# One decoder layer on one core: small TensorE products moved inside dense matmul pieces, a routing step with other instructions and an index table converted in two parts

## Chip, cores and metric

The kernel is written for one Trainium2 chip and runs on one of its cores. The metric is the time of one execution on the device, in microseconds (us); a kernel's time is the median of its runs. TensorE is called PE here, VectorE DVE, ScalarE ACT, GpSimd POOL and SyncE SP. "fp32r" is TensorE's one-pass format for 32-bit numbers; plain fp32 products take two recorded instructions each.

## The reference, cut to what matters

One layer over 1088 tokens (1024 of a prompt, 8 x 8 of a decoding batch), width 1024: a projection into eight groups of 256 columns, four mixers, an output projection with residual, then a routed mixture of 32 experts of which each token uses two.

```python
h = rmsnorm(x, g_mix)
z = h @ w_in                                  # 1024 -> 2048
a_b, a_c, a_x, p_x, c_a, c_g, d_u, d_v = split(z, 8)
y_a = a_b * causal_dwconv(a_c * a_x, state_a, conv_a_w)       # 3 taps
y_p = multiscale_pool(p_x, ...)               # causal means over 2, 4, 8, 16 rows, minus x, then 64x64 products, times pool_scale
y_c = silu(layernorm(causal_dwconv(c_a * sigmoid(c_g), state_c, conv_c_w) + b))   # 31 taps
y_d = d_u * chunk_spatial_mix(layernorm(d_v)) # 128 x 128 causal product per chunk and head
x = x + concat([y_a, y_p, y_c, y_d]) @ w_out
h = rmsnorm(x, g_ffn)
# hier_moe: top group of 4, then top 2 of its 8 experts
lg = h @ rg_w + rg_b;  p_top, g_idx = top_k(softmax(lg), 1)
le_sel = (h @ re_w + re_b).reshape(n, 4, 8)[g_idx]
v2, e_idx = top_k(le_sel, 2);  w2 = softmax(v2) * p_top
x = x + sum_k w2[k] * (silu(h @ w_gate[e_k]) * (h @ w_up[e_k])) @ w_down[e_k]
y = rmsnorm(x, g_final)
```

The last rows of the inputs of mixers A, B and C, and the normed v rows of mixer D, are outputs too (the "states").

## The kernel before, in words

Each engine has one program, in an order written out by hand; semaphores join them, and every engine works strictly in its own order. Tokens are cut in nine tiles of 128 rows (the last has 64).

**Input projection.** The weight matrix comes in 16 pieces of 128 columns, in the order of the list PIECES: cg0, ca0, cg1, ca1, v0, v1, du0, du1, p0, p1, ac0, ax0, ac1, ax1, ab0, ab1. For each piece SP loads it, ACT copies the high part (`part_hi`), DVE computes the low part (`part_lo`), and PE runs `z(p)`: 8 steps over the contraction, each of 9 matmuls (three products of high and low parts, three ranges of tokens), 72 in all. A `behind` function, if there is one, is called after each of the 8 steps. ACT or DVE empties the result (`empty`, `glu`, `a_input`, `a_gate`), and `z(p)` can only start when the piece two before in the same banks has been emptied.

**Small work between the pieces.** Spatial products of mixer D (`spatial`, nine, behind the steps of `z(9)`), transposes of the states (`tails`, which need ACT's `tail_copy`), pool products (`pool_product`, three ranges for each of two channel halves c), channel means and variances of mixer C (`over_channels`), all in plain fp32. They share two PSUM banks in the order of the list M_USES: a product may open its bank when the product two before it in the list has been read out. DVE meanwhile computes the 31-tap convolution of mixer C, one instruction of 1024 columns per tap (`taps_c(c, k0, k1)`, line 1148), the pool sums (`pooled(c)`: running sums, a selection, then means minus input) and, for the second channel half, `sample_c(1)`; `conv_ready` is signalled after them.

**Output projection and router phase.** Weights of the output are split in the same way (`part_hi`, `part_lo` of NPIECE + c). PE's loop runs i over tiles: the first half of `project(i)` (24 matmuls of 512 columns), transposes of normed tile i-1, the running counts `cum` of tile i-2 (two fp32 products of 32 columns: `upper` and `ones` times `msum`), the second half, the router logits of tile i-1 (8 fp32 products of 40 columns), and `table_add(i-2)`. DVE does `mix_lo`, `places`, `table_parts`, `residual`, `normed`, `route`. `route` picks group and experts by MAX8 and FIND_INDEX8; `places` gives each token its row in the expert's list; `table_parts` makes the factors from which `table_add` builds the table of token indices, 32 experts by 9 columns, in PSUM. After the last addition DVE turns the table to integers (lines 1444 to 1446), signals `idx_ready`, and POOL starts the first gather.

**Experts and end.** SP loads three weight blocks at once, after the last normed tile, and the others once the third gather has landed. PE takes block after block: transposes of the gathered tokens, gate and up products, a transpose, down products; at most 16 extra blocks follow for experts with over 128 tokens (three with this data). POOL gathers and scatters. At the end DVE adds the two gated rows of each token and norms.

## Time and profile before

| | us |
|---|---|
| median of 3 runs | 693.06 |
| lowest, highest | 691.35, 695.70 |
| the profiled execution | 691.8 |
| its span in the profile | 690.0 |
| PE busy in the span | 585.3 (85%) |
| DVE busy | 371.3 (54%) |
| ACT busy | 203.4 (29%) |
| POOL busy | 97.1 (14%) |

The profiled execution's time is 1.8 us above its span and 1.26 us under the median. Busy shares are averages over stages: input projection to about 258 us, output projection and router to about 406 us, experts to 636 us, then the final sums. Times in the rows are counted from the start of the span.

### The profile page before, as it was taken

The page shows a single profiled execution, that of the slowest core. Times are in us where ns is not written, and L with a number is a line of the kernel's source. Part 1 is how long each engine was busy: PE and PEld are TensorE (multiplying, and loading weights), DVE is VectorE, ACT ScalarE, POOL GpSimd, SP SyncE. Part 2 cuts the span into 40 slices and gives each one's busy share as a digit, 9 for nine tenths or more (in the row PEclk, how much of TensorE's full clock was granted, in tenths as well). Part 3 has the DMA queues.
Part 4 walks back from the last instruction along what each step waited for, and adds up shares of the span by engine and source line. Part 5 has one row for each costly group of instructions (what it writes and reads, how often), then busy time and mean ns, then how long its engine had stood idle before and what let it go on. Part 6 is the DMA issues. An engine that isn't in the chain of part 4 may idle for free. (4 is left out here: it accounts for less than half of the span.)

```text
span 690.0 us, 9547 instructions
## 1 busy us (share of the span) xinstructions
PE 585.3 (85%) x3149; PEld 498.7 (72%) x3149; DVE 371.3 (54%) x668; ACT 203.4 (29%) x349; POOL 97.1 (14%) x150
## 2 busy tenths in 40 slices
PE   3899999994999998999999629999999999998000
PEld 2899999972998896888887417777777787775000
DVE  4929988999993676466566570111111111111497
ACT  6632113220323263211311103333333333332232
POOL 4300002000000000000000211233232333231000
PEclk9999999997999999999999758999999999999555
DMA  9623111120223333100010368998899999892694
GB/s 320 122 93 65 44 32 30 53 60 0 62 79 121 115 108 123 62 30 32 31 61 32 120 228 265 336 327 294 303 340 315 344 326 360 295 334 100 260 352 167
DMA packets 51439, 116.27 MB, mean 169 GB/s; under 512 B 8434, under 2 KB 26743, under 8 KB 50295
## 3 DMA queue, kind: packets, MB, share of 16 engines
q1 hardware_dynamic: 42899, 92.82, 39.8%
q0 software_dynamic: 6656, 17.84, 7.3%
q10 hardware_dynamic: 1828, 4.96, 2.0%
q8 instruction: 25, 0.41, 0.3%
q14 instruction: 31, 0.25, 0.1%
HBM read 99.75 MB, written 20.68 MB: 175 GB/s over the span
## 5 line engine op out<-in xcount | busy, mean ns | idle before, releaser
L1600 PE MATMUL ps<-at_hT,at_ring 128*128 128x384 f32 x936 | 160.3, 330 | 0.0
L1600 PEld LDWEIGHTS ps<-at_hT,at_ring 128*128 128x128 f32 x936 | 155.5, 188 | 1.2 <-issue 1.2
L1833 PE MATMUL ps<-at_wexp,at_hTm 128*128 128x256 f32 x560 | 128.0, 382 | 0.0
L1833 PEld LDWEIGHTS ps<-at_wexp,at_hTm 128*128 128x128 f32 x560 | 104.6, 192 | 13.3 <-issue 0.3
L1756 PE MATMUL ps<-at_hT,at_mring 128*128 128x512 f32 (+1 forms) x432 | 102.3, 392 | 2.4 <-DVE at_mring L1300 1.7
L1756 PEld LDWEIGHTS ps<-at_hT,at_mring 128*128 128x128 f32 (+1 forms) x432 | 77.4, 182 | 21.5 <-issue 2.1
L1479 DVE TENSOR_TENSOR at_actv<-at_sg,ps 128x128 f32<-128x128 f32 x35 | 10.0, 287 | 148.6 <-ACT at_sg L832 148.6
L1148 DVE SCALAR_TENSOR_TENSOR at_mixT<-at_uc,sb_par,at_mixT 128x1024 f32<-128x1024 f32 x60 | 77.4, 1289 | 2.1
L1853 PE MATMUL ps<-at_wexp,at_actT 128*128 128x512 f32 x140 | 65.9, 593 | 0.9 <-ACT at_actT L840 0.9
L1819 PEld LDWEIGHTS ps<-sb_ident,at_xg 128*128 128x128 f32 x280 | 37.4, 193 | 26.2 <-issue 22.5
L543 ACT ACTIVATE at_wk<-at_x 128x1024 f32<-128x1024 f32 (+1 forms) x27 | 28.6, 1058 | 85.0 <-DVE at_x L1353 52.4
L1819 PE MATMUL ps<-sb_ident,at_xg 128*128 128x128 f32 x280 | 38.8, 284 | 9.3 <-DMA at_xg<-scratch_h,at_gidxs 7.9
L1487 DVE COPY at_outb<-ps 128x512 f32<-128x512 f32 x35 | 24.2, 691 | 41.5 <-PE ps L1853 41.5
L1023 POOL DMA_INDIRECT scratch_out<-at_outb,at_tab x32 | 30.4, 948 | 103.1 <-DVE at_outb L1487 99.6
L825 ACT ACTIVATE at_hTm<-ps 128x1024 f32<-128x1024 f32 x35 | 35.8, 1024 | 18.5 <-PE ps L1819 18.5
L1853 PEld LDWEIGHTS ps<-at_wexp,at_actT 128*128 128x128 f32 x140 | 26.5, 190 | 20.0 <-issue 16.7
L1091 DVE SCALAR_TENSOR_TENSOR at_wk<-at_x,sb_rs,sb_gain 128x1024 f32<-128x1024 f32 (+1 forms) x18 | 23.1, 1284 | 31.6 <-POOL sb_rs L926 24.9
L1008 POOL DMA_INDIRECT at_xg<-scratch_h,at_gidxs x32 | 31.6, 989 | 54.2 <-issue 37.3
L924 POOL TENSOR_SCALAR sb_ss<-sb_ss 128x1 f32<-128x1 f32 (+1 forms) x18 | 5.2, 290 | 231.4 <-ACT at_wk L543 231.1
L1556 PE MATMUL ps<-sb_ident,at_wk 128*128 128x128 f32 (+1 forms) x144 | 23.6, 318 | 16.2 <-DVE at_wk L1091 12.4
L849 ACT ACTIVATE at_outb<-ps 128x512 f32<-128x512 f32 x35 | 20.9, 597 | 52.0 <-PE ps L1853 52.0
L1556 PEld LDWEIGHTS ps<-sb_ident,at_wk 128*128 128x128 f32 (+1 forms) x144 | 21.2, 200 | 19.1 <-issue 13.3
(214 smaller groups left out, 580.3 us busy)
## 6 DMA issues: line engine op xcount, KB each, us to landing
at_wexp<-in_expert_w_gate SPq DMA_DIRECT2D x35, 512.0 KB, 7.4
at_wexp<-in_expert_w_up SPq DMA_DIRECT2D x35, 512.0 KB, 4.5
at_wexp<-in_expert_w_down SPq DMA_DIRECT2D x35, 512.0 KB, 6.0
at_x<-in_x_prompt SPq DMA_DIRECT2D x16, 512.0 KB, 6.1
at_raw<-in_w_in SPq DMA_DIRECT2D x16, 512.0 KB, 4.1
at_opair<-scratch_out SPq DMA_DIRECT2D x8, 1024.0 KB, 11.8
scratch_h<-at_wk SPq DMA_DIRECT2D x8, 512.0 KB, 2.6
out_y_prompt<-at_x ACTq DMA_DIRECT2D x8, 512.0 KB, 3.2
```

Of the source, the lines that this page charges most:

```text
L543: do(A(wk[0:n, 2, 0:D], x1[0:n, i, :], ACT.Square, accum_out=ss[0:n, norm, i:i + 1]), s["sq_done"])
L825: nc.scalar.activation(hTm[:, j % 2, :, :], src, ACT.Copy).then_inc(s["htm_ready"], 1)
L1008: g.indirect_dma_start(xg[0:n, b % XG, :], None, hs, bass.IndirectOffsetOnAxis(ap=index[0:n, :], axis=0), bounds_check=last_token, oob_is_ ...
L1023: g.indirect_dma_start(orow, bass.IndirectOffsetOnAxis(ap=index[0:n, :], axis=0), outb[0:n, b % 2, :], None, bounds_check=last_pair, oob_i ...
L1148: do(stt(y, x, par[:, c, k:k + 1], y, ALU.mult, ALU.add))
L1487: v.tensor_copy(outb[:, j % 2, 512:D], ps[:, 6, :]).then_inc(s["ob_dve"], 1)
L1556: mm = pe.transpose(ps[:, banks + k // 4, k % 4 * P:k % 4 * P + n], wk[0:n, i % 2, 0:D].rearrange("p (q k) -> p k q", k=KC)[:, k, :], iden ...
L1600: mm = pe.matmul(ps[:, bank + r, 0:t1 - t0], w[:, wpart, k * P:(k + 1) * P], hT[:, hpart, k, t0:t1], start=(m, wpart, hpart) == (0, 0, 0), ...
L1756: mm = pe.matmul(ps[0:n, b + r, :], mring[:, 1 - i % 2, mpart, k * P:k * P + n], wo[:, wpart, k, r * 512:(r + 1) * 512], start=(c, mpart, ...
L1819: mm = pe.transpose(ps[:, k // 4, k % 4 * P:(k % 4 + 1) * P], xg[:, j % XG, :].rearrange("p (q k) -> p k q", k=KC)[:, k, :], ident[:])
L1833: mm = pe.matmul(ps[:, 2 + j % 2, 0:2 * FF].rearrange("p (g f) -> p g f", g=2), hTm[:, j % 2, k, :], w[:, :, k, :], start=k == 0, stop=k = ...
L1853: mm = pe.matmul(ps[:, 5 + r, :], actT[:, j % 2, :], wexp[:, j % LAP, q:q + 512], start=True, stop=True)
```

## The change

- PE: pool products, state transposes, means and variances are no longer issued between the pieces, but by `behind` functions after given steps of z(10), z(12), z(13), z(14) and z(15). Their order among themselves is the same.
- DVE: `pooled(c)` is cut in `pool_sums` and `pool_means`. For c = 0 both move up between the spatial steps; only three taps stay there (13 to 15) instead of eight; taps 16 to 19 come before the second pool, 20 to 30 after it.
- PE: `project` is cut in four quarters. In iterations before the last the order is that of before. In the last one (tile 8) the logits of tile 7 come between the third and the fourth quarter; after the loop: counts of tile 7, transposes, logits of tile 8, table of 7, counts of 8, table of 8.
- DVE: in the last iterations `route(7)` comes before `residual(8)`, `places(7)` right after it, `table_parts(7)` ahead of `route(8)`.
- `route`: instead of multiplying by the group's one-hot and reducing to 8 values, it adds -1e30 to the other groups and takes MAX8 and FIND_INDEX8 over all 32; one reduction and one index computation go.
- Counts: `upper`, `msum` and a new copy `ones_r` (made by POOL after output-weight part 3) are fp32r, so that the two count products are one-pass.
- The table is converted in two parts: the first three experts' 27 columns, with a signal, then the other 261; POOL waits for the second before its fourth gather.

```diff
-        upper = sb("upper", [P, P])
+        upper = sb("upper", [P, P], F32R)
-        msum = sb("msum", [P, 2, NE])
+        msum = sb("msum", [P, 2, NE], F32R)
...
+            lo_wait(pool, NPIECE + 3)
+            do(g.tensor_copy(ones_r[:], ones[:]), s["ones_ready"])
...
+                if b == 0:
+                    pool.wait_ge(s["idx_ready"], 2)
...
-            zf_wait(dve, "du1")
-            for i in range(TILES):
-                spatial(i)
-                if i < LAST:
-                    taps_c(1, 13 + i, 14 + i)
-            def pooled(c):
-                n = HP + NP + SB * (HP + ST)
-                row = [wk[:, r, :] for r in range(3)]
+            def pool_rows(c):
+                return [wk[:, n, :] for n in range(3)], HP + NP + SB * (HP + ST)
+            def pool_sums(c):
...
+                return dst
+            def pool_means(c, dst):
...
-            pooled(0)
+            zf_wait(dve, "du1")
+            spatial(0)
+            spatial(1)
+            taps_c(1, 13, 14)
+            spatial(2)
+            sums = pool_sums(0)
+            spatial(3)
+            spatial(4)
+            pool_means(0, sums)
+            spatial(5)
+            spatial(6)
+            taps_c(1, 14, 15)
+            spatial(7)
+            taps_c(1, 15, 16)
+            spatial(LAST)
             part_lo(11)
-            taps_c(1, 21, 24)
+            taps_c(1, 16, 20)
             part_lo(12)
-            pooled(1)
-            taps_c(1, 24, 31)
+            pool_means(1, pool_sums(1))
+            taps_c(1, 20, 31)
...
-                do(ts(goh[q, :], io4[q, :], gidx[q, :], None, ALU.is_equal))
+                do(ts(goh[q, :], io4[q, :], gidx[q, :], -1.0e30, ALU.not_equal, ALU.mult))
                 le = lge[q, i, 8:].rearrange("p (g e) -> p g e", g=NG)
                 do(tt(rjunk[q, :].rearrange("p (g e) -> p g e", g=NG), le,
-                      goh[q, :].unsqueeze(2).broadcast_to([n, NG, EG]), ALU.mult))
-                do(v.tensor_reduce(sel8[q, :], rjunk[q, :].rearrange("p (g e) -> p e g", g=NG), AX_X,
-                                   ALU.add))
-                do(v.max(n8[q, i, :], sel8[q, :]))
-                do(v.max_index(j8[q, :], n8[q, i, :], sel8[q, :]))
-                do(ts(sc[q, 2:3], gidx[q, :], float(EG), None, ALU.mult))
-                do(ts(eidx[q, z, :], j8[q, 0:2], sc[q, 2:3], None, ALU.add))
+                      goh[q, :].unsqueeze(2).broadcast_to([n, NG, EG]), ALU.add))
+                do(v.max(n8[q, i, :], rjunk[q, :]))
+                do(v.max_index(j8[q, :], n8[q, i, :], rjunk[q, :]))
+                do(v.tensor_copy(eidx[q, z, :], j8[q, 0:2]))
...
             for i in range(TILES + 2):
                 if i + 1 < TILES:
                     mix_lo(i + 1)
-                if i >= 2:
+                if i == TILES:
+                    table_parts(i - 2)
+                elif i >= 2:
                     places(i - 2)
-                    if i < TILES:
-                        table_parts(i - 2)
+                    table_parts(i - 2)
+                if i == LAST:
+                    route(i - 1)
                 if i < TILES:
                     residual(i)
+                    if i == LAST:
+                        places(i - 1)
                     dve.wait_ge(s["rs_ready"], TILES + i + 1)
                     if i >= 2:
                         dve.wait_ge(s["t2_done"], i - 1)
                         dve.wait_ge(h2_stored[i % 2], 16 * (i // 2))
                     normed(i, 1, "h2_ready")
-                if 1 <= i <= TILES:
+                if 1 <= i <= TILES and i != LAST:
                     route(i - 1)
-                if i >= TILES:
-                    table_parts(i - 2)
             dve.wait_ge(s["table_added"], TILES)
-            do(ts(empty[:], ps[:, 7, 0:TCOLS], 0.0, float(NONE + 1), ALU.is_equal, ALU.mult))
-            do(stt(tab[:], empty[:], -1.0, ps[:, 7, 0:TCOLS], ALU.add, ALU.add))
-            do(ts(gidxs[:], tab[:], 1, None, ALU.logical_shift_right), s["idx_ready"])
+            for c0, c1 in ((0, 3 * CAPB), (3 * CAPB, TCOLS)):
+                do(ts(empty[:, c0:c1], ps[:, 7, c0:c1], 0.0, float(NONE + 1), ALU.is_equal, ALU.mult))
+                do(stt(tab[:, c0:c1], empty[:, c0:c1], -1.0, ps[:, 7, c0:c1], ALU.add, ALU.add))
+                do(ts(gidxs[:, c0:c1], tab[:, c0:c1], 1, None, ALU.logical_shift_right), s["idx_ready"])
...
+            def pool_product(c, r):
...
+            def behind_ac0(m):
+                if m == 0:
+                    pe.wait_ge(s["px_ready"], 1)
+                    tails("pst0", wk[:, 0, :], HP, HP)
+                if m in (2, 3, 4):
+                    pool_product(0, m - 2)
+            def behind_ac1(m):
+                if m == 0:
+                    pe.wait_ge(s["px_ready"], 2)
+                    tails("pst1", wk[:, 0, :], HP, HP)
+                if m in (5, 6, 7):
+                    pool_product(1, m - 5)
+            def behind_ax1(m):
+                if m in (2, 4, 6):
+                    r = m // 2 - 1
+                    pe.wait_ge(s["conv_ready"], 1)
+                    over_channels("mean", r, mixT[:, 4:6, LN_RANGES[r][0]:LN_RANGES[r][1]])
+            def behind_ab0(m):
+                if m == 0:
+                    pe.wait_ge(s["ua_ready"], 1)
+                    tails("ast0", wk[:, 0, :], HA, HA)
+                if m in (2, 3, 4):
+                    r = m - 2
+                    pe.wait_ge(s["c_sq"], r + 1)
+                    over_channels("var", r, lnsq2[:] if r == 2 else lnsq[:, r, :, :])
+            def behind_ab1(m):
+                if m == 4:
+                    pe.wait_ge(s["ua_ready"], 2)
+                    tails("ast1", wk[:, 1, :], HA, HA)
+            z(10, behind=behind_ac0)
+            z(11)
+            z(12, behind=behind_ac1)
+            z(13, behind=behind_ax1)
+            z(14, behind=behind_ab0)
+            z(15, order=WO, behind=behind_ab1)
...
+            def second_T(t):
+                pe.wait_ge(s["h2_ready"], t + 1)
+                if t >= 1:
+                    pe.wait_ge(s["h2T_ready"], t)
+                transposes(t, 4).then_inc(s["t2_done"], 1)
+            def counts(t):
+                n = rows(t)
+                b = m_open(f"cum{t}")
+                pe.wait_ge(s["m_onehot"], t + 1)
+                pe.wait_ge(s["ones_ready"], 1)
+                pe.matmul(b[0:n, 0:NE], upper[0:n, 0:n], msum[0:n, t % 2, :], start=True, stop=True)
+                pe.matmul(b[:, NE:2 * NE], ones_r[0:n, :], msum[0:n, t % 2, :], start=True, stop=True)\
+                    .then_inc(s["m_ready"], 1)
+            def logits(t):
+                n = rows(t)
+                b = m_open(f"lg{t}")
+                pe.wait_ge(s["h2T_ready"], t + 1)
+                pe.wait_ge(s["late_in"], 16 * 8)
+                for k in range(KC):
+                    mm = pe.matmul(b[0:n, 0:8 + NE], h2T[:, t % 2, k, 0:n], rw[:, k, :],
+                                   start=k == 0, stop=k == KC - 1)
+                mm.then_inc(s["m_ready"], 1)
+            for i in range(TILES):
+                project(i, 0)
+                project(i, 1)
+                if i >= 1:
+                    second_T(i - 1)
                 if i >= 2:
-                    t = i - 2
-                    n = rows(t)
-                    b = m_open(f"cum{t}")
-                    pe.wait_ge(s["m_onehot"], t + 1)
-                    pe.matmul(b[0:n, 0:NE], upper[0:n, 0:n], msum[0:n, t % 2, :], start=True, stop=True)
-                    pe.matmul(b[:, NE:2 * NE], ones[0:n, :], msum[0:n, t % 2, :], start=True, stop=True)\
-                        .then_inc(s["m_ready"], 1)
-                if i == TILES + 1:
-                    table_add(LAST - 1)
-                if i < TILES:
-                    project(i, 1)
-                if 1 <= i <= TILES:
-                    t = i - 1
-                    n = rows(t)
-                    b = m_open(f"lg{t}")
-                    pe.wait_ge(s["h2T_ready"], t + 1)
-                    pe.wait_ge(s["late_in"], 16 * 8)
-                    for k in range(KC):
-                        mm = pe.matmul(b[0:n, 0:8 + NE], h2T[:, t % 2, k, 0:n], rw[:, k, :],
-                                       start=k == 0, stop=k == KC - 1)
-                    mm.then_inc(s["m_ready"], 1)
-                if 2 <= i < TILES:
+                    counts(i - 2)
+                project(i, 2)
+                if i == LAST:
+                    logits(i - 1)
+                project(i, 3)
+                if 1 <= i < LAST:
+                    logits(i - 1)
+                if i >= 2:
                     table_add(i - 2)
+            counts(LAST - 1)
+            second_T(LAST)
+            logits(LAST)
+            table_add(LAST - 1)
+            counts(LAST)
             table_add(LAST)
```

## Rows read from the trace of the kernel before

**Rows 1.** Page: busy tenths of 40 slices of 17.25 us, granted clock.

```profile
PE   3899999994999998999999629999999999998000
...
DVE  4929988999993676466566570111111111111497
...
PEclk9999999997999999999999758999999999999555
```

**Rows 2.** Timeline of PE at the pool products: start us, us, instructions, idle before.

```profile
160.72 0.45 PE L1681 MATMUL ps<-sb_wsb,at_vall 64*64 64x64 f32 x8 [1.37 <-DVE sb_sptmp L1210]
...
165.97 0.47 PE L1662 MATMUL ps<-sb_ident,sb_sptmp 128*120 128x128 f32 x1 [2.66 <-ACT sb_sptmp L600]
170.78 3.88 PE L1701 MATMUL ps<-at_wk,sb_pw 128*128 128x512 f32 x6 [4.34 <-DVE sb_sc L1257]
174.47 12.23 PE L1600 MATMUL ps<-at_hT,at_ring 128*128 128x384 f32 x72
```

**Rows 3.** Windows of 2 us, PE: length, busy, granted clock, DMA share.

```profile
164.00:166.00 2.00, 0.03 (x1) 0.51 0.00 0
...
174.00:176.00 2.00, 2.00 (x12) 0.93 0.72 215
```

**Rows 4.** Timeline of DVE, 147 to 240 us.

```profile
149.05 0.42 DVE L1210 TENSOR_TENSOR sb_sptmp<-ps,sb_biasd 128x256 f32<-128x256 f32 x1
...
165.56 1.43 DVE L1243 TENSOR_TENSOR at_wk<-at_wk 128x1222 f32<-128x1222 f32 x1
...
170.76 1.23 DVE L1108 TENSOR_TENSOR at_ring<-at_raw,at_ring 128x1024 fp32r<-128x1024 f32 x1
...
178.06 4.36 DVE L1243 TENSOR_TENSOR at_wk<-at_wk 128x1222 f32<-128x1222 f32 x3 [0.85 <-ACT sb_acts L704]
...
186.20 9.21 DVE L1148 SCALAR_TENSOR_TENSOR at_mixT<-at_uc,sb_par,at_mixT 128x1024 f32<-128x1024 f32 x7
...
202.08 1.68 DVE L1276 TENSOR_TENSOR at_wk<-ps,at_mixT 128x768 f32<-128x768 f32 x3
...
236.57 3.35 DVE L1325 RECIPROCAL at_lnsq<-at_lnsq 128x512 f32<-128x512 f32 x1
```

**Rows 5.** Timeline of ACT, 250 to 253 us.

```profile
250.77 0.56 ACT L557 ACTIVATE sb_stage<-ps 2x128 f32<-2x128 f32 x2
...
252.08 1.06 ACT L569 ACTIVATE at_hT<-at_wo_x 128x1024 fp32r<-128x1024 f32 x1 [0.74 <-PE ps L1600]
```

**Rows 6.** Timeline of PE, means to projection.

```profile
212.93 3.98 PE L1716 MATMUL ps<-at_mixT,sb_avg 128*128 128x512 f32 x12
...
257.83 8.37 PE L1756 MATMUL ps<-at_hT,at_mring 128*128 128x512 f32 x36
267.90 2.97 PE L1756 MATMUL ps<-at_hT,at_mring 128*128 128x512 f32 x12 [1.70 <-DVE at_mring L1300]
...
306.31 0.39 PE L1787 MATMUL ps<-sb_msum,sb_ones 128*128 128x32 f32 x2
```

**Rows 7.** Timeline of PE, end of the router phase.

```profile
388.81 1.14 PE L1556 MATMUL ps<-sb_ident,at_wk 64*128 64x64 f32 x8 [2.90 <-DVE at_wk L1091]
...
399.85 0.39 PE L1786 MATMUL ps<-sb_msum,sb_upper 64*64 64x32 f32 x2 [3.15 <-DVE sb_msum L1382]
...
412.56 1.94 PE L1819 MATMUL ps<-sb_ident,at_xg 128*128 128x128 f32 x8 [6.97 <-DMA at_xg<-scratch_h,at_gidxs]
```

**Rows 8.** Timeline of DVE, end of the router phase.

```profile
391.37 0.20 DVE L1373 TENSOR_REDUCE sb_sel<-sb_rjunk 128x8 f32<-128x32 f32 x1
...
396.81 0.19 DVE L1364 TENSOR_TENSOR sb_stage<-ps,sb_rb 64x40 f32<-64x40 f32 x1 [0.64 <-PE ps L1801]
...
405.70 0.46 DVE L1444 TENSOR_SCALAR at_empty<-ps 128x288 f32<-128x288 f32 x1 [1.01 <-PE ps L1769]
```

**Rows 9.** Timeline of SP's queue: issues.

```profile
403.61 0.43 SPq L494 DMA_DIRECT2D at_wexp<-in_expert_w_down  x1
```

**Rows 10.** Gathers of line 1008: from issue to landing.

```profile
DMA to landing us min/median/max: 3.5/5.9/9.3
```

More of the change, by code:

```diff
@@ L184, in build_layer @@
         pcol = at("pcol", [P, 2, TCOLS], o_raw + 2 * P * 4, F32R)
+        ones_r = at("ones_r", [P, P], o_raw + 2 * P * 4 + 2 * TCOLS * 4, F32R)
         empty = at("empty", [P, TCOLS], o_raw + 2 * P * 4)
@@ L1249, in pooled @@
                        ALU.mult, ALU.add))
+                return dst
+            def pool_means(c, dst):
+                row, n = pool_rows(c)
                 d = row[1 + c]
@@ L1696, in pool_product @@
                 prompt, sample = work(wk[:, 1 + c, :], HP)
-                for r, (t0, t1) in enumerate(LN_RANGES):
-                    b = m_open(f"pm{c}{r}")
-                    x = sample if r == 2 else prompt[:, t0:t1]
-                    y = b[:, 0:NS].rearrange("p (b t) -> p b t", b=SB) if r == 2 else b
-                    pe.matmul(y, pw[:, c, :], x, start=True, stop=True).then_inc(s["m_ready"], 1)
-            pool_product(0)
-            z(10)
-            pe.wait_ge(s["px_ready"], 2)
-            tails("pst1", wk[:, 0, :], HP, HP)
-            z(11)
-            pool_product(1)
-            z(12)
+                t0, t1 = LN_RANGES[r]
+                b = m_open(f"pm{c}{r}")
+                x = sample if r == 2 else prompt[:, t0:t1]
+                y = b[:, 0:NS].rearrange("p (b t) -> p b t", b=SB) if r == 2 else b
+                pe.matmul(y, pw[:, c, :], x, start=True, stop=True).then_inc(s["m_ready"], 1)
             def over_channels(what, r, src):
@@ L1717, in over_channels, with project @@
                 mm.then_inc(s["m_ready"], 1)
-            pe.wait_ge(s["conv_ready"], 1)
-            for r, (t0, t1) in enumerate(LN_RANGES):
-                over_channels("mean", r, mixT[:, 4:6, t0:t1])
-            z(13)
-            pe.wait_ge(s["ua_ready"], 1)
-            tails("ast0", wk[:, 0, :], HA, HA)
-            for r in range(3):
-                pe.wait_ge(s["c_sq"], r + 1)
-                over_channels("var", r, lnsq2[:] if r == 2 else lnsq[:, r, :, :])
-            z(14)
-            pe.wait_ge(s["ua_ready"], 2)
-            tails("ast1", wk[:, 1, :], HA, HA)
-            z(15, order=WO)
-            def project(i, half):
+            def behind_ac0(m):
[33 more added lines that the diff above has]
+            z(15, order=WO, behind=behind_ab1)
+            def project(i, q):
                 n = rows(i)
                 b = 2 * (i % 2)
-                if half == 0:
+                if q == 0:
                     if i == 0:
@@ L1747, in project @@
                         pe.wait_ge(s["x1_ready"], i - 1)
-                for c in range(half * KC // 2, (half + 1) * KC // 2):
+                for c in range(q * KC // 4, (q + 1) * KC // 4):
                     k = WO[c]
@@ L1759, in project @@
                                            stop=(c, mpart, wpart) == (KC - 1, 1, 0))
-                if half == 1:
+                if q == 3:
                     mm.then_inc(s["o_done"], 1)
```

15 lines of the change are left out of this document (2 added, 13 removed).

## The prediction

> **What bounds the kernel now.** I read the page's slices first. PE is at 9 of 10 in nearly every slice up to the router phase, but drops to 4 in one slice (155 to 172 us) and to 6, 2 and 9 around 380 to 414 us, while DVE is at 9 in the first hole and at 5 to 7 in the second [rows 1]. Those two holes are where this change works. Then PE's timeline around the first hole: waits of 1.37, 2.66 and 4.34 us, and one more of 1.9 between the first two, until piece z(10) starts at 174.47 [rows 2]. In that hole the granted clock went from 1.00 to half, 1.2 GHz, at 164 us, and came back at about 174, after 3.4 us of pool products without a pause [rows 2, 3]; I price a fall at about 1.8 us, half the 3.88 us that those products took. From 174.47 on PE runs z(10) to z(15) nearly without a gap and enters the projection at 257.83; there it waits 1.70 us for DVE's last low parts, at 267.90 [rows 6]. In the second hole PE waits for the normed last tile (2.90), for routing (3.15) and for the first gather (6.97) [rows 7].
>
> **First hole, new order.** PE works the same products, so PE time is moved, not removed. I walk DVE, PE and ACT from 146.8, where DVE begins `spatial(0)`; it takes 0.91 per spatial step (0.42 for its first half [rows 4], the second alike, and the gaps), 1.32 per tap (9.21 for seven [rows 4]), 5.20 for pool 0 (165.56 to 170.76 [rows 4]: 2.97 of sums, the rest means). Eight full spatial steps, three taps, the pool and the last half-size step end at 164.05 (before: 165.5). PE has its last spatial product at 159.3 instead of 160.72, and z(10) starts at 160.0 instead of 174.47, with the means input already done at 157.9. A piece takes 12.1 (72 matmuls, 12.23 with the last one's tail [rows 2]), a step of it 1.51.
>
> What is late next: the transpose behind z(10)'s first step needs ACT's copy, which needs the last spatial step (the wait of 2.66 in [rows 2]). Copy and handover put it at 164.5, so PE stops from 161.75 to 164.5: 2.75 us, with the seven other steps of z(10) queued behind it. Then steps 1 to 4 with three pool products between (0.86, 0.86, 0.1 at full clock: half of [rows 2]'s rate for six instructions) end at 172.6, z(10) at 177.2. z(11) to 189.3, z(12) with its 2.0 of products and transposes to 203.6.
>
> DVE after 164.05: low part 11 (1.23 [rows 4]), four taps, low part 12, to 171.8. Then it waits for the second pool's input: ACT must first read out the third pool product (173.0), then copies in 2.3 us; that copy is what DVE's 0.85 before 178.06 ended on [rows 4]. DVE so starts pool 1 at 175.4 instead of 178.06 [rows 4], but has eleven taps behind it instead of seven: from there to `conv_ready` 22.7 us before (it is 1.3 before 202.08, low part 13 between), 28.0 now, and `a_input(0)`, which before began at 202.08 [rows 4] and ended at 203.8, ends at 206.35. z(13) needs it: PE waits 2.7 and starts z(13) at 206.4. Before, z(13) began 3.8 after 212.93 [rows 6], at 216.7.
>
> z(13) carries the means (3.8 in all, from 3.98 busy for twelve instructions [rows 6]) to 222.3; low part 14 now stands behind the third mean on DVE and is ready at 222.45, a tie. z(14) with its variances ends at 238.4, z(15) at 250.7 (before 257.8): PE has gained 7.1. But the path leaves PE here. The variance chain on DVE (reciprocals of 3.35 [rows 4]) started at 236.57 and starts at 231.0, and ACT's SiLU ends at 245.2 instead of 250.7. ACT then must read out the transpose behind step 4 of z(15), at 246.1; before it read it at 250.77 [rows 5] with no wait. So the first output-weight split starts at 247.5 instead of 252.08 [rows 5]: 4.6 gained. Everything that `project(0)` needs last hangs on this split: the low parts, the weight loads 5 to 7 that reuse its buffers, `a_gate(1)`, and the matmuls at 267.90 [rows 6], which now start at 263.2 after a PE wait of 3.8. SP's other loads stay early enough: output weight 3 is issued after low part 14, 2.6 later than before, but 25 us ahead of its use. **Term: -4.6.** Bounds: -7.1 if the split chain did not bind, -3 if ACT's queue costs another step.
>
> **Loop.** Quarters change nothing before the last tile. The counts are 4 instructions in 0.36 us (306.17 to 306.53; the last of them in [rows 6]), 0.09 each; one-pass makes 2 of them. I take 0.18 saved, in six iterations: **-1.1** (none if setting up weights is all the cost, -2 at most). The FP8 and Floating Point Precision page of the Trainium skill, section TensorE Precision Notes, says that plain fp32 makes four passes; by that rule alone a one-pass count saves three quarters, and the term would be -1.6. `route` loses the reduction (0.20 [rows 8]) and one index step and pays for longer searches: 0.4 shorter, hidden behind PE for tiles 0 to 6. POOL's `ones_r` copy waits for low part 3 at about 254 and stands ahead of the first router norm at 270: nothing.
>
> **Second hole** (times of the old trace, before the shifts above). `logits(7)` (1.70) now lies before the last quarter. So the last projection ends 1.5 later, at 385.2, and residual, square, root and norm bring the last normed tile to 390.25 instead of 388.75 (PE took it at 388.81 [rows 7]); POOL's memset and SP's first weight loads move with it. But `route(7)` and `places(7)` are done by then, in the wait for the norm. Transposes, ACT's 0.6 and `logits(8)` at low clock (1.9) let `route(8)` start at 394.15 instead of 396.81 [rows 8]: -2.65. It is 0.4 shorter. After it, counts, places, table factors and addition ran from 399.85 [rows 7] to the conversion at 405.70 [rows 8], with 1.5 of tile 7's table factors in between, which are now done before; one-pass counts at low clock take about 0.65: -0.95. Conversion: three instructions over 288 columns took 1.3; over 27 columns I take 0.65 (small DVE operations are near 0.2 [rows 8]): -0.65. The second part, 1.2, is over before the fourth gather, some 7 us later. Together 4.65 for the first gather's issue.
>
> It does not all arrive. The first gather was issued at 407.9 and its tokens were used at 412.56 [rows 7], when SP's queue had gone quiet: the last of the three early weight blocks was issued at 403.61 [rows 9] and has about 4 us of data. Now that issue comes 1.5 later and the gather 4.65 earlier, so they share the DMA engines. Gathers under load land in 5.9 us (median), 3.5 to 9.3 [rows 10], against about 4.5 here. I take 1.7 lost. **Term: -2.95** (between -4.65 and 0 at the slowest landing).
>
> The expert stage I shift as a whole: its weight stream resumes on the third gather, and PE runs it back to back but for single gathers that come late. So the sum is 4.6 + 1.1 + 2.95 = 8.65 us. From the profiled execution, 691.8 (span 690.0 and 1.8 around it), that gives 683.15; that execution lies 1.26 below the median of the three runs, which I halve: **683.8 us**, 1.3% below 693.06. One per cent, 6.9 us, is about what a measurement of this kernel can tell from no change.
>
> **The rivals.**
> *The clock falls in the new gaps.* The new order has PE stop inside dense work for 2.75, 2.7 and 3.8 us. Against a fall: 1.70 before 267.90 [rows 6] left the clock near 1.00 in its slice, the sixteenth [rows 1]. For it: after 2.90 us before 388.81 [rows 7] it fell, though there PE had done only 40- and 288-column products just before, and in the first hole hardly anything for 5 us. Each fall costs 1.8: all three give 689.2. The Trainium skill, page TensorE: Matmul & The Clock Gate, section The HAM clock gate, has an idle array drop to half rate whatever surrounds the gap; by that rule this rival is as likely as my forecast for the longest gap, and that alone would give 685.6. I take no fall, since dense matmuls stand on both sides. Chance of two or more: 0.18.
> *The experts take it back.* The tail's gain is spent on late gathers or the weight stream's end: 8.65 - 2.95 = 5.7 left, 686.7. For it: at most 9.3 us for one gather [rows 10]. Chance 0.08.
> *Slower: z(10) runs at 1.2 GHz.* The clock falls at the first wait (161.75) and the waits behind steps 2 to 4 for ACT keep it low, so that a piece takes 24.2 instead of 12.1. The gain is gone when 0.7 of one piece runs so; with one and a half pieces it is 683.8 + 18 = 702. Against it: the three products' banks are read out well within a step (1.5 us). Chance 0.04.
> *The change does less than it says*, PE still waits for the same things: in z(11) if the second pool's input were later. Only an early z(10) with no gain beyond it, 691; chance 0.04.
> *More is won*: gathers uncontended and the experts' late gather (about 2 us) gone: 679.5; it lies in my forecast's spread.
>
> **How the numbers follow.** Forecast with its spread 0.66, 680 to 686. Range 679.5 to 689.3: it takes in the uncontended gathers below and three clock falls above. Faster by over 1% (below 686.1): 0.68, the forecast's cases and a little of the rivals; within 1%: 0.28; slower: 0.04.
>
> **What would show it.** z(10) begins near 160 and PE stops once behind its first step; z(13) waits for `a_input(0)` and starts near 206; projection's first matmul near 251, its seventh step near 263 after the longest PE wait of the stage. In the loop 14.1 us a tile instead of 14.3. `route(7)` ends before `residual(8)` begins; from the last projection matmul to the first gather's issue 18 us instead of 24. Granted clock 1.00 from 160 to about 380. I am wrong if the clock shows halves inside z(10) to `project(0)`, if z(13) waits for something other than `a_input(0)`, or if the expert stage is longer than before.

## The result and the profile after

The changed kernel takes 690.92 us (median of 20 runs, 687.56 to 699.26), the kernel before 695.01 (20 runs beside them, 691.35 to 698.51). The ratio is 0.995, 95% interval 0.9926 to 0.9974: 3.5 us faster, 1.8 to 5.1. The forecast was 683.8 with a range of 679.5 to 689.3, so it promised more than twice the gain and its range missed the result. The profiled execution took 692.34 (span 690.6), against 691.8 (690.0) before: by the one profile each, nothing seems gained. Most of what follows therefore stands on medians and ratios, and the traces tell where the time goes. A ratio leaves out runs in the chip's slower state (here those over 1.5% above the fastest of their kernel), a median takes in all.

The page after, where it differs from [rows 1]: the busy slices of PE, its clock, and the chain that ended last.

```profile
PE   3999999998989998999999429999999999997000
...
PEclk9999999999999999999999759999999999999555
...
DMA 31%; DVE 6%; issue 3%; SPq 2%; PE 2%; POOLq 0%; ACT 0%; POOL 0%; DVEq 0%; ACTq 0%
```

The first hole is nearly gone: a slice of 4 with a clock of 0.7 has become an 8 with a clock of 0.9, with a second 8 two slices on. The second hole is 4 and 2 instead of 6 and 2, since it begins earlier, and the clock is back at 0.9 a slice sooner. The chain that ended last went 28% through PE before; now 31% of it is DMA, nearly all of it the experts' `w_down`.

PE after, from z(10)'s first step to the transposes of the first projection tile; it answers to [rows 2] and [rows 6].

```profile
160.20 1.76 PE L1621 MATMUL ps<-at_hT,at_ring 128*128 128x384 f32 x9
...
164.92 0.34 PE L1683 MATMUL ps<-sb_ident,sb_sptmp 128*120 128x128 f32 x1 [2.66 <-ACT sb_sptmp L600]
165.00 4.77 PE L1621 MATMUL ps<-at_hT,at_ring 128*128 128x384 f32 x18
...
208.62 6.25 PE L1621 MATMUL ps<-at_hT,at_ring 128*128 128x384 f32 x27 [3.29 <-DVE at_wk L1296]
...
255.48 8.42 PE L1799 MATMUL ps<-at_hT,at_mring 128*128 128x512 f32 x36 [0.40 <-issue]
266.46 10.07 PE L1799 MATMUL ps<-at_hT,at_mring 128*128 128x512 f32 x36 [2.57 <-DVE at_mring L1320]
276.38 1.06 PE L1577 MATMUL ps<-sb_ident,at_wk 128*128 128x128 f32 x8
```

z(10) starts at 160.20 instead of 174.47, 14.3 us earlier. The three waits that the forecast walked out (2.75, 2.7, 3.8) are there as 2.66, 3.29 and 2.57. But look at what stands behind them: two steps of z(10) need 4.6 us where a step needs 1.5, three steps of z(13) 6.1 where they need 4.6, and the 36 matmuls from the projection's seventh step on 9.9 where 36 need about 8.4. The windows of PE say why (length, busy, granted clock, DMA share).

```profile
163.00:165.00 2.00, 0.08 (x1) 1.00 0.00 0
...
166.00:168.00 2.00, 2.00 (x8) 0.50 0.38 113
...
210.00:212.00 2.00, 2.00 (x9) 0.50 1.02 399
...
268.00:270.00 2.00, 2.00 (x6) 0.50 0.04 12
```

After each of the three gaps the granted clock went from 1.00 to 0.50, from 2.4 to 1.2 GHz, for 3 to 3.5 us. Dense matmuls on both sides did not prevent it.

What DVE and ACT show of the same stretch, against [rows 4] and [rows 5]:

```profile
177.50 4.36 DVE L1244 TENSOR_TENSOR at_wk<-at_wk 128x1222 f32<-128x1222 f32 x3 [5.23 <-ACT sb_acts L704]
...
206.80 1.68 DVE L1296 TENSOR_TENSOR at_wk<-ps,at_mixT 128x768 f32<-128x768 f32 x3
...
251.99 1.06 ACT L569 ACTIVATE at_hT<-at_wo_x 128x1024 fp32r<-128x1024 f32 x1 [0.74 <-ACT sb_stage L557]
```

Pool 1 began at 177.50 (178.06 before; forecast 175.4), `a_input(0)` at 206.80, and the first output-weight split at 251.99, 0.1 before its old time where 4.6 were promised. The transposes of the first projection tile are issued at 276.38, against 277.13 before. So 14.3 us at z(10) have become 0.75 at the first tile's end. One execution does not fix such a number well: three kernels below (with the stream late, the stream early, and block 0 moved) have this same front, and their first tile's transposes are issued at 276.19, 278.41 and 277.53.

The tail does what was forecast up to the gathers. PE after, against [rows 7]:

```profile
388.05 1.14 PE L1577 MATMUL ps<-sb_ident,at_wk 64*128 64x64 f32 x8 [4.44 <-DVE at_wk L1095]
...
394.86 0.26 PE L1829 MATMUL ps<-sb_msum,sb_upper 64*64 64x32 f32 x1 [2.06 <-DVE sb_msum L1399]
...
408.56 1.95 PE L1877 MATMUL ps<-sb_ident,at_xg 128*128 128x128 f32 x8 [8.85 <-DMA at_xg<-scratch_h,at_gidxs]
```

DVE at the end of the router phase, against [rows 8]:

```profile
392.13 0.19 DVE L1384 TENSOR_TENSOR sb_stage<-ps,sb_rb 64x40 f32<-64x40 f32 x1 [0.47 <-PE ps L1840]
...
399.82 0.18 DVE L1465 TENSOR_SCALAR at_empty<-ps 128x27 f32<-128x27 f32 x1 [1.01 <-PE ps L1812]
```

And the gathers' issues on POOL, and SP's first issue of the resumed weight stream:

```profile
401.36 1.31 POOL L1010 DMA_INDIRECT at_xg<-scratch_h,at_gidxs  x1 [11.03 <-DVE at_gidxs L1467]
403.61 1.25 POOL L1010 DMA_INDIRECT at_xg<-scratch_h,at_gidxs  x1 [0.94 <-issue]
405.89 0.94 POOL L1010 DMA_INDIRECT at_xg<-scratch_h,at_gidxs  x1 [1.04 <-issue]
```

```profile
413.74 0.33 SPq L494 DMA_DIRECT2D at_wexp<-in_expert_w_gate  x1
```

`route(8)` begins 4.7 us earlier, the conversion 5.9, the first gather's issue 6.55. Its tokens are used 4.0 earlier (408.56 against 412.56). The stream, which waits for the third gather, resumes 2.5 earlier (it did at 416.20), since that gather took 7.8 us from its issue to SP's resuming instead of 3.8. That time stands for its landing below.

### The profile page after: what moved, and what is told of

The parts are those of the page before. It is cut to its first block and busy times, and to the rows that moved or that the text cites. A ratio compares the mean times of both kernels' runs of the same rounds, so it can differ in the third digit from the quotient of the medians.

```text
span 690.6 us, 9513 instructions
## 1 busy us (share of the span) xinstructions
PE 586.7 (85%) x3131; PEld 500.4 (72%) x3131; DVE 369.5 (54%) x653; ACT 203.5 (29%) x349; POOL 98.8 (14%) x151
## 5 line engine op out<-in xcount | busy, mean ns | idle before, releaser
L1621 PE MATMUL ps<-at_hT,at_ring 128*128 128x384 f32 x936 | 168.8, 338 | 3.6 <-DVE at_wk L1296 3.3
L1621 PEld LDWEIGHTS ps<-at_hT,at_ring 128*128 128x128 f32 x936 | 158.9, 191 | 9.2 <-issue 8.4
L1799 PE MATMUL ps<-at_hT,at_mring 128*128 128x512 f32 (+1 forms) x432 | 103.9, 397 | 3.0 <-DVE at_mring L1320 2.6
L1911 PEld LDWEIGHTS ps<-at_wexp,at_actT 128*128 128x128 f32 x140 | 26.5, 190 | 19.9 <-issue 16.7
L832 ACT ACTIVATE at_sg<-ps 128x128 f32<-128x128 f32 x35 | 9.7, 278 | 86.7 <-PE ps L1891 74.8
```

The lines of the kernel that those rows point to most:

```text
L1621: mm = pe.matmul(ps[:, bank + r, 0:t1 - t0], w[:, wpart, k * P:(k + 1) * P], hT[:, hpart, k, t0:t1], start=(m, wpart, hpart) == (0, 0, 0), ...
L1799: mm = pe.matmul(ps[0:n, b + r, :], mring[:, 1 - i % 2, mpart, k * P:k * P + n], wo[:, wpart, k, r * 512:(r + 1) * 512], start=(c, mpart, ...
L1911: mm = pe.matmul(ps[:, 5 + r, :], actT[:, j % 2, :], wexp[:, j % LAP, q:q + 512], start=True, stop=True)
```

## The experiments

All are compared with the kernel before, run on the same chip beside them.

**The two halves of the change, each alone.** The first kernel is the one before with only the new order of pieces and pool products on PE and DVE; the second is the changed kernel with that part put back.

> Only the input-projection part of the change (products behind the steps of the pieces, pool sums between the spatial steps); the router phase as before. Theory 1 (the granted clock falls in each new PE gap and costs about 1.5 us each, three times): the second projection tile starts only about 0.8 us earlier than before, as in the whole change, and the kernel is 0 to 1 us faster. Rival (my prediction's term): 4.6 us faster.

> Only the router-phase part (routing, one-pass counts, quarters, table in two parts); the input projection as before. The first gather is issued about 5.8 us earlier in both theories. Theory 2 (the stream of expert weights sets the end of the expert stage, and it resumes on the third gather's landing): gathers share the DMA engines with the early weight blocks, the third lands only 1.5 to 2.5 us earlier, and the kernel is about 2 us faster. Rival (PE runs the experts back to back and sets the end): the first transposes come 3.3 us earlier and the kernel is 3.3 us faster.

Pieces alone: 695.71 us (12 runs) against 692.86, ratio 0.9995 (0.9957 to 1.0032; by the medians alone it would be 1.004, but the means, 695.0 and 694.4, are 1.001 apart, and the runs before spread up to 700). Router part alone: 690.79 (12 runs), ratio 0.9944 (0.991 to 0.9978), 3.9 us faster (1.5 to 6.2). The second has all of the change's gain. In its trace the first gather's tokens are used 3.6 us earlier and the stream resumes only 1.1 earlier (415.09); 3.9 is nearer the rival's 3.3 than theory 2's 2, but the interval holds both. PE in the first:

```profile
165.46 0.33 PE L1678 MATMUL ps<-sb_ident,sb_sptmp 128*120 128x128 f32 x1 [2.66 <-ACT sb_sptmp L600]
...
209.15 6.25 PE L1616 MATMUL ps<-at_hT,at_ring 128*128 128x384 f32 x27 [3.32 <-DVE at_wk L1292]
...
267.82 8.47 PE L1793 MATMUL ps<-at_hT,at_mring 128*128 128x512 f32 x29 [3.37 <-DVE at_mring L1316]
```

The same three gaps, three low clocks behind them (0.55, 0.65 and 0.50 in windows of 2 us), and the seventh step at its old time, 267.82. The first tile's transposes are 0.6 later than before (277.72), not 0.8 earlier as expected. The term of -4.6 is refuted as a whole: it measured -0.35, between -3.0 and +2.2.

**The gaps filled.** The changed kernel with matmuls added whose results nobody reads, 13, 17 and 9 of them, one group in each gap. Nothing is left out.

```diff
+            def fill(n, out, rhs):
+                for _ in range(n):
+                    pe.matmul(out, upper[:], rhs, start=True, stop=True)
...
+            b = m_open("mean0")
+            fill(17, b[:, 0:384], hT[:, 0, 7, 0:384])
             z(13, behind=behind_ax1)
```

> The whole change plus dummy fp32r matmuls, overwritten later, in the three new PE gaps: 13 of 384 columns before the first pool transposes, 17 of 384 before z(13), 9 of 512 before the seventh step of the first projection tile. They fill the gaps without removing the waits. Theory 1: the clock stays at 2.4 GHz in all three places, z(13) starts 1.6 us earlier, z(14) 3.1 us earlier, the second projection tile about 4.5 us earlier, and the kernel is about 4 us faster than the change. Rival (the loss is in the order of the queues): nothing moves, the same time as the change.

```profile
164.70 0.33 PE L1683 MATMUL ps<-sb_ident,sb_sptmp 128*120 128x128 f32 x1 [0.33 <-ACT sb_sptmp L600]
...
206.86 4.74 PE L1621 MATMUL ps<-at_hT,at_ring 128*128 128x384 f32 x27 [0.28 <-DVE at_wk L1296]
...
265.03 3.04 PE L1808 MATMUL ps<-at_hT,at_mring 128*128 128x512 f32 x12 [2.29 <-DVE at_mring L1320]
...
274.34 1.06 PE L1577 MATMUL ps<-sb_ident,at_wk 128*128 128x128 f32 x8
```

```profile
165.00:168.00 3.00, 3.00 (x20) 1.00 0.28 83
209.00:212.00 3.00, 3.00 (x18) 1.00 1.00 400
267.00:270.00 3.00, 2.30 (x10) 1.00 0.01 3
```

```profile
248.71 1.06 ACT L569 ACTIVATE at_hT<-at_wo_x 128x1024 fp32r<-128x1024 f32 x1 [0.74 <-ACT sb_stage L557]
```

With something running in the gaps the clock stays at 1.00 in all three places, z(13) starts at 206.86 (forecast for a kernel without falls: 206.4) and takes 4.6 for its three steps. The falls, and their 1.6 us each in z(10) and z(13), are caused by the gaps. ACT's first split of output weights starts at 248.71, 3.3 earlier than in the change. But T(0), the transposes of the first tile, come only 2.04 earlier (274.34), not 4.5 as theory 1 had it: ACT's last split waits for output weights that land later (two waits of 1.51 and 1.87 us instead of 0.49 and 0.95), and the third fall had cost only 0.6 there, since a wait of 0.70 for DVE follows where it is gone. The first gather is issued 1.94 earlier, but its tokens take 11.6 us, and the stream resumes at 413.99, no earlier than in the change. The median is 690.9 (12 runs, ratio 0.9944, 0.9905 to 0.9983), where theory 1 had 4 us less: no gain that can be seen beyond the change. Two microseconds are within these intervals, so this run shows the falls, not what they are worth at the end.

**What the end hangs on.** The changed kernel, with SP waiting for the sixth gather instead of the third before it resumes the weight stream.

```diff
-            sp.wait_ge(gath[2], 16)
+            sp.wait_ge(gath[1], 32)
```

> The whole change, but the expert weight stream resumes on the sixth gather instead of the third, some 5 us later; nothing else is touched. Theory 2: the end moves with the stream, 4 to 5 us slower than the change, with PE waiting for weights in more blocks. Rival (PE sets the end): block 3 is used 20 us after its load, so the delay is absorbed: 0 to 1 us slower.

```profile
412.56 0.93 POOL L1010 DMA_INDIRECT at_xg<-scratch_h,at_gidxs  x1 [3.62 <-PE ps L1877]
427.50 0.96 POOL L1025 DMA_INDIRECT scratch_out<-at_outb,at_tab  x1 [14.00 <-DVE at_outb L1508]
429.48 1.00 POOL L1010 DMA_INDIRECT at_xg<-scratch_h,at_gidxs  x1 [1.02 <-issue]
```

The sixth gather stands behind the first scatter on POOL, so the delay was 19.9 us (resume at 433.65), four times what was meant. The kernel took 707.65 (6 runs), 16.7 more than the change's median and 15.8 by the ratios, ratio 1.0178 (1.0123 to 1.0233), and PE waited 10.4 us for `w_down` in four places. By these numbers the stream has 3 to 4 us of slack against PE; the intervals allow a few us either way. The opposite, resuming on the first gather (`gath[0]`), was sent later with the next group:

> The whole change, but the weight stream resumes on the first gather instead of the third. Theory 2: it resumes near 408.5 instead of 413.7 and the kernel is 3 to 5 us faster than the change, as the stream 20 us later cost 16.7. Rival: the second and third gather are slowed by the stream and the gain is gone, 0 to 2 us slower.

It took 690.96 (12 runs, ratio 0.9938, 0.9905 to 0.9971), 0.8 us under the change by the ratios and no gain that can be seen. In its profiled execution the front is 2 us late, so times count from the first gather's issue at 403.40: the stream resumed 6.4 us behind it (409.78) instead of 12.4, but now ran over the second gather, whose tokens were used 10.6 us after its issue at 405.65 instead of 9.0.

```profile
409.90 1.94 PE L1877 MATMUL ps<-sb_ident,at_xg 128*128 128x128 f32 x8 [8.15 <-DMA at_xg<-scratch_h,at_gidxs]
416.21 1.94 PE L1877 MATMUL ps<-sb_ident,at_xg 128*128 128x128 f32 x8 [4.37 <-DMA at_xg<-scratch_h,at_gidxs]
```

**Gathers without weight loads beside them.** The changed kernel, with expert block 0's three loads issued ahead of the last tile's store, so that the early blocks are through sooner.

```diff
             for i in range(TILES):
+                if i == LAST:
+                    sp.wait_ge(s["o_done"], TILES)
+                    expert_block(0, 0, 0, first=True)
                 sp.wait_ge(s["h2_ready"], i + 1)
...
-            for j in range(3):
+            for j in range(1, 3):
```

> The whole change, but SP issues the three loads of weight block 0 as soon as the last projection is done, ahead of the store of the last normed tile, which comes 5 us later. Theory 2: the early blocks end 3 to 5 us earlier, so the gathers find the DMA engines freer, the third lands near 410, and the kernel is 2 to 4 us faster than the change. Rival (the gathers' time is their own, not that of the weights ahead of them): they land when they did, same time.

```profile
402.52 1.31 POOL L1012 DMA_INDIRECT at_xg<-scratch_h,at_gidxs  x1 [11.04 <-DVE at_gidxs L1469]
...
407.05 0.94 POOL L1012 DMA_INDIRECT at_xg<-scratch_h,at_gidxs  x1 [1.04 <-issue]
```

```profile
406.99 1.95 PE L1879 MATMUL ps<-sb_ident,at_xg 128*128 128x128 f32 x8 [6.12 <-DMA at_xg<-scratch_h,at_gidxs]
```

First gather 4.5 us from issue to use instead of 7.2, third gather 3.7 us to its landing (SP resumes at 410.71) instead of 7.8: the contention is the early weight blocks'. The time is 690.3 (13 runs, ratio 0.9926, 0.9899 to 0.9954), 1.7 us below the change by the ratios, whose intervals overlap; the profiled execution was the slowest of its runs (697.0), with 9.0 us of waits for weights in the experts, and its late part is no guide.

**The gaps closed by order.** The changed kernel, rearranged so that each short product stands where its input is there: the transposes of the pool's state two steps later and the pool products one step later in z(10), four more taps ahead of pool 1 so that DVE works while ACT copies, and mixer A's last state transposes behind z(14)'s last step instead of z(15)'s fifth.

```diff
-                if m == 0:
+                if m == 2:
                     pe.wait_ge(s["px_ready"], 1)
                     tails("pst0", wk[:, 0, :], HP, HP)
-                if m in (2, 3, 4):
-                    pool_product(0, m - 2)
+                if m in (3, 4, 5):
+                    pool_product(0, m - 3)
...
-            taps_c(1, 16, 20)
+            taps_c(1, 16, 24)
...
-            taps_c(1, 20, 31)
+            taps_c(1, 24, 31)
```

> The whole change with its waits moved out of PE's way: first pool transposes behind the third step of z(10) instead of the first, pool products one step later, four more taps ahead of the second pool, the last state transpose of mixer A behind the last step of z(14). Theory 1: no PE gap over 1.2 us and no fall of the clock between 150 and 250 us; z(13) starts near 203 instead of 208.6, z(15) ends near 249 instead of 255, the second projection tile starts 4 to 6 us earlier than in the change. Theory 2: hardly any of that reaches the end; the third gather still lands near 413, and the kernel is 0 to 2 us faster than the change. Rival (PE sets the end of the experts): 4 to 6 us faster than the change.

```profile
164.85 0.32 PE L1683 MATMUL ps<-sb_ident,sb_sptmp 128*120 128x128 f32 x1
...
203.36 4.74 PE L1621 MATMUL ps<-at_hT,at_ring 128*128 128x384 f32 x27 [2.65 <-DVE at_wk L1296]
...
258.95 10.08 PE L1800 MATMUL ps<-at_hT,at_mring 128*128 128x512 f32 x36 [2.38 <-DVE at_mring L1320]
```

```profile
203.00:205.00 2.00, 1.64 (x10) 1.00 1.00 304
...
261.00:263.00 2.00, 2.00 (x7) 0.50 0.04 12
```

687.5 us (6 runs), ratio 0.9854 (0.9788 to 0.992): 6.7 below the change by the ratios. This ratio rests on four runs; the means of all six give 0.9885, 4.5 below. z(13) starts 5.3 us sooner, T(0) 7.5 sooner (268.86), the first gather's issue 7.5 sooner, the stream's resume 7.1 sooner. Most of a shift at the front arrives; the theory that hardly anything of it reaches the end was wrong. So was theory 1's "no PE gap over 1.2 us": z(13) still waits 2.65. The last gap still costs a fall (36 matmuls in 10.08 instead of 8.4). z(13)'s gap of 2.65 cost none here. It did in the next kernel, the same but for the edits of the two stream experiments:

> The edits of the three runs before in one kernel. Theories 1 and 2 together: the clock stays up, the front is 4 to 6 us earlier and the stream resumes at once, so that both reach the end: 8 to 12 us faster than the change, near 680. If the sum is less than 5 us, something third sets the end.

```profile
203.33 7.46 PE L1623 MATMUL ps<-at_hT,at_ring 128*128 128x384 f32 x27 [2.66 <-DVE at_wk L1298]
```

```profile
204.00:205.00 1.00, 1.00 (x4) 0.50 1.16 367
```

The same wait to a hundredth, and here the clock fell, shortly before PE went on, and three steps took 7.3 us instead of 4.6: 2.7 lost. This kernel took 680.75 (6 runs), ratio 0.9769 (0.9723 to 0.9815). So the two stream edits, which gain 0.8 and 1.7 by the ratios when made alone to the change, gave 5.9 on top of the closed gaps; the intervals of the two ratios (0.9854, 0.9769) meet at 0.979 to 0.982, so the size of this is not firm.

**z(13)'s gap closed too, and the pieces alone again.** On DVE, low part 13 and `a_input(0)` ahead of the sampled taps: once in the kernel with everything, and once with the closed pieces only on top of the kernel before, nothing of the router's part and nothing of the stream's.

```diff
+            part_lo(13)
+            a_input(0, 11)
             sample_c(1)
             do(v.tensor_copy(sc[:, 7:8], ones[:, 0:1]), s["conv_ready"])
-            part_lo(13)
...
-            a_input(0, 11)
             a_taps(0)
```

> The edits of e8_all_together, and on DVE low part 13 and a_input(0) stand ahead of the sampled taps, so that z(13) has its input before PE has finished z(12). Theory 1 (PE's gap ahead of z(13), 2.66 us in both runs, is all that is left of the new gaps and costs a clock fall besides in some executions): z(13) starts at about 200.7 instead of 203.3 without a wait, the clock stays at 1.00 there, T(0) is issued 2.6 us sooner than in e5 (about 266.2) and in e8 as profiled 5.3 us sooner, and the time is about 677.5, 2.6 to 5 us under e8's 680.75. Rival (the path to project(0) has left PE for DVE and ACT there: variance chain, SiLU, split of output weights): z(13) starts sooner, but T(0) stays at about 268.9 and the time at 680 to 681.

> The kernel before with only the new order of pieces, its gaps closed as in e5 and e9 and nothing of the router's part. Theory 1 (the pieces part failed in e1 only for its gaps and their clock falls; a shift at the front arrives in full at the end): T(0) at about 266 instead of 277.1, and the time 9 to 11 us under the kernel before, about 684.5, ratio 0.985. Rival (early pieces are worth little by themselves, since the second hole or the weight stream takes the gain back; e5's gain needed the router's part): at most 4 us under the kernel before, 691 or more.

Everything: 677.36 us (6 runs, 674.48 to 682.58), ratio 0.9747 (0.9707 to 0.9788), by the ratios 1.5 us under the kernel that still waits at z(13); these intervals overlap. Pieces alone: 684.47 (6 runs) against 693.75, ratio 0.9858 (0.9812 to 0.9903), 9.9 us faster (6.7 to 13.0). PE in the first of them:

```profile
201.11 4.72 PE L1623 MATMUL ps<-at_hT,at_ring 128*128 128x384 f32 x27
...
256.64 10.06 PE L1802 MATMUL ps<-at_hT,at_mring 128*128 128x512 f32 x36 [2.35 <-DVE at_mring L1319]
```

```profile
259.00:261.00 2.00, 2.00 (x6) 0.50 0.01 4
```

z(13) follows z(12) without a wait at 201.11, 7.5 earlier than in the change, with no fall. T(0) is issued at 266.54 and, with the pieces alone, at 266.32: 10.8 before its old time, of which 9.9 show at the end. That is the part of the change that measured -0.35 when its products stood where their inputs were not yet ready, with the moves named above. Most of the difference is waits and not falls: against the first version of the pieces alone T(0) is 11.4 us sooner (it was 277.72), while the two falls that are gone had cost 1.6 each. One gap is left, ahead of the seventh step (2.35, and 2.79 with the pieces alone), and it costs a fall in both.

## Why the prediction was wrong

The direction held, the size did not: 8.65 us were forecast and 3.5 (1.8 to 5.1) measured.

*First hole, -4.6 forecast, -0.35 measured alone. This is where it failed*, and first of all at one sentence: "I take no fall, since dense matmuls stand on both sides." The gaps were forecast to within 0.1 us for the first, 0.6 short for the second and 1.2 long for the third. Each cost a fall of about 1.6 us by the traces (each was priced at 1.8), and the filled gaps show the cause. They also compound with the rest of the walk. The fall in z(10) brought the third pool product later, with it pool 1 (2.1 late) and `a_input(0)` (2.1 late: it begins at 206.80 instead of about 204.65); z(13) so started 2.2 late and lost 1.6 more; ACT, which must read out a transpose of z(15) before it splits the output weights, was 4.5 late, and nothing of the 4.6 was left there. That step, from PE to ACT, was right: the split hangs on z(15)'s transpose as written.

The falls are not the whole of it. In the kernel with filled gaps ACT's split is 3.3 us earlier, so 1.2 of the 4.5 are small sizes of the walk: z(13) starts 0.5 later than forecast even so, and the rest comes between z(13) and z(15), 0.3 of it a wait for low part 14, which the walk had as a tie. Another 0.6 is in the landing of the output weights. At the first tile the term would have been -2.8 without falls, not -4.6; with them it was -0.75 (one execution each, of a front that moves by 2 us between executions). And no run shows at the end what the falls alone cost.

The bounds given for the term, -7.1 to -3, did not hold zero, since the falls were kept out of them and put with a rival. That rival (all three falls, 689.2, chance 0.18) is what happened. That its sum, 3.9 us under 693.06, comes so near the measured 3.5 is in part luck: it charges 5.4 us for three falls, and the filled gaps gave back 2.0 at the first tile.

What weighed wrongly was the evidence for it. The gap of 1.70 before [rows 6] was taken to speak against a fall at 2.7, and the fall at 2.90 before 388.81 [rows 7] was explained away by thin products in front of it. The nearest rows in length were right: none at 1.70, a fall at 2.90, and at 2.57, 2.66 and 3.29 here. The section The HAM clock gate of the Trainium skill's page TensorE: Matmul & The Clock Gate has an idle array drop to half rate whatever surrounds the gap. The trace agrees for these three gaps between dense matmuls. A gap of 2.65 us, in the kernel with the gaps closed by order, passed without a fall, so a gap's length alone does not tell. The prediction cited the section and chose against it.

*Loop, -1.1 forecast.* T(0) moved by 0.75 and T(7) (374.61 against 376.89) by 2.28, so seven periods gave 1.5, 0.22 each where 0.18 was taken. Right; the counts themselves give 0.13, and they start 0.08 sooner behind the transposes (0.80 us from their start instead of 0.88).

*Tail, -2.95 forecast.* With the loop 4.05, and the router part alone measured 3.9 (1.5 to 6.2). From T(7) to the first gather's issue the path is 4.3 shorter (4.65 forecast), and 2.6 of it were lost in the gathers instead of 1.7. The cause given for the loss, early weight blocks beside the gathers, is shown by moving block 0. The forecast also passed over a row of the kernel before: there `route(7)`'s one-hot instruction on DVE took 1.43 us instead of 0.23, beside POOL's memset, and it stands in the profile's chain of work that ended last; the new order takes `route(7)` out from beside the memset, and by these rows about 1.2 us of this part's gain may be that (an estimate; nothing tried it). In its place tile 7's table factors took 2.70 us instead of 0.6 beside the memset, but they lay in a wait.

*The expert stage shifts as a whole.* Borne out for the front's shifts, within wide intervals (7.5 in at T(0) and 6.7 out, 10.8 in and 9.9 out). What carries a shift to the end was not settled. "PE runs it back to back" holds only by 3 to 4 us, since the stream 19.9 us late cost about 16; but the stream 6 us sooner behind the first gather gained nothing that can be seen. In the change the stream's resume moved by 2.5, the first tokens by 4.0, and the median by 4.1.

*The clock* was to be 1.00 from 160 to 380; it was not. *More is won* (679.5; its own terms, 1.7 and about 2, give 680.1) and *slower* (702) did not occur. *The experts take it back* may hold a microsecond of the rest: runs of one kernel differ by 5 us and more, and intervals of 2.5 us and up can't split that further.

## What to carry to other kernels

A short product put inside dense matmuls saves its own gap only if its input is there when PE comes to it; otherwise it moves the gap to where PE was dense, and the chip adds a clock fall. So place it a step or two late, and compare each wait that remains with those that cost a fall here (2.35 us and longer, with one exception). Closing two of three such gaps, with DVE's order changed for it, turned a part worth nothing into 9.9 us. And when a walk through several engines has a "no fall" in it, run the walk once with the fall before the term gets its bounds: here most of what the walk lost hung on that sentence.

## What the runs showed of the hardware

The clock after a gap inside dense matmuls: at 1.70 us it stayed at 1.00, and at 2.29, with nine added matmuls just ahead of it, it stayed too. At 2.65, ahead of z(13), it stayed in one kernel, and at 2.66 it fell in the next with the same order and times. At every other gap in the three places (2.35 to 3.85 us long, in nine traces) it fell. The half rate then lasted about 3.4 us and cost 1.3 to 1.6, but twice it lasted some 6.8 us, with PE busy for all but its first 0.8 us, and cost 2.7 and 2.8 (after the 2.66, and after the 3.85 in the kernel with the stream on the first gather). What decides between these was not tried.

The third gather, an indirect one of 128 rows, landed in 3.6 to 3.8 us where the early weight blocks were through (the kernel before, the pieces alone with gaps closed, block 0 moved) and in 7.8 to 10.0 beside them (the change, the router part alone, the gaps filled, the gaps closed).

DVE's two tensor-scalar instructions of 128x128 beside POOL's memset in the change, and one of 128x4 in the kernel before:

```profile
386.81 3.52 POOL L1033 MEMSET at_xg<- 128x4096 f32 x1 [0.20 <-POOL sb_rs L926]
```

```profile
388.03 2.70 DVE L1429 TENSOR_SCALAR at_prow<-sb_wsT,sb_row 128x128 fp32r<-128x128 f32 x2
...
397.30 0.59 DVE L1429 TENSOR_SCALAR at_prow<-sb_wsT,sb_row 64x128 fp32r<-64x128 f32 x2
```

```profile
387.57 3.52 POOL L1031 MEMSET at_xg<- 128x4096 f32 x1 [0.20 <-POOL sb_rs L926]
```

```profile
389.69 1.43 DVE L1368 TENSOR_SCALAR sb_goh<-sb_io,sb_gidx 128x4 f32<-128x4 f32 x1
```

The pair ends at 390.73, 0.4 behind the memset's end at 390.33, and the same pair for the last tile, with POOL idle, takes 0.59. The instruction of 128x4 ends at 391.12, with the memset (391.09), and takes 0.22 to 0.23 for the tiles before and after. Eight traces read for it have the one or the other: 1.43 us where `route(7)` meets the memset (three), 2.70 where the table factors do (five). `route(7)`'s other instructions ran beside the memset at their usual times. That the memset holds these instructions is read from such rows; no run here took the memset away.
